# Two transformer blocks on one core: the start reordered, with the input laid out by feature and the small vectors as ready columns

## The reference

```python
def rms_norm(x, g):
    xf = x.astype(jnp.float32)
    y = xf * lax.rsqrt(jnp.mean(xf * xf, axis=-1, keepdims=True) + EPS)
    return (y * g.astype(jnp.float32)).astype(x.dtype)

hn = rms_norm(x, norm_mix_g[0])
gate, xr = jnp.split(hn @ rec_w_in, 2, axis=-1)
xpad = jnp.pad(xr, ((0, 0), (CONV_W - 1, 0), (0, 0)))
xc = conv_b + xpad[:, 0:S] * conv_w[0]
for k in range(1, CONV_W):
    xc = xc + xpad[:, k:k + S] * conv_w[k]
# then gates r, i from xc @ w_a, xc @ w_x, a scan over time, times gelu(gate), @ w_out
```

## Time and profile before

| | |
|---|---|
| median of 3 runs | 1874.32 us (1873.71 to 1875.22) |
| the profiled execution | 1874.16 us |
| its span | 1872.8 us, so 1.36 us lie around it |
| TensorE busy | 1859.4 us, 99% |
| VectorE, ScalarE, GpSimd busy | 979.5, 675.3, 377.3 us |
| DMA | 172.36 MB, mean 92 GB/s |
| granted TensorE clock | 0.999 |

### The profile page before, as it was taken

One profiled execution on the slowest core, in us unless ns is written; L12 is line 12 of the kernel. 1 busy time (PEld: TensorE's weight loads), 2 busy tenths in 40 slices (PEclk: granted clock), 3 DMA queues, 4 the chain that ended last, 5 costly groups with the idle time before them and its releaser, 6 DMA issues.

```text
span 1872.8 us, 21950 instructions
## 1 busy us (share of the span) xinstructions
PE 1859.4 (99%) x8944; PEld 1508.1 (81%) x8944; DVE 979.5 (52%) x1324; ACT 675.3 (36%) x915; POOL 377.3 (20%) x337
## 2 busy tenths in 40 slices
PE   9999999999999999999999999999999999999998
PEld 8888888888877568888888879788787888888887
DVE  7885543334458864543434356666446454443433
ACT  6753322222234772321212234555323332222213
POOL 2004210010336793210101131111001311110102
PEclk9999999999999999999999999999999999999999
DMA  4322323322333103223223232222232322233221
GB/s 160 113 90 90 113 90 101 101 90 93 104 96 96 63 1 113 91 90 112 91 90 109 80 98 84 68 68 68 85 118 80 110 93 90 90 100 103 90 96 62
DMA packets 167171, 172.36 MB, mean 92 GB/s; under 512 B 7480, under 2 KB 164288, under 8 KB 167072
## 3 DMA queue, kind: packets, MB, share of 16 engines
q1 hardware_dynamic: 164576, 163.76, 27.3%
q0 software_dynamic: 2496, 7.21, 1.2%
HBM read 168.69 MB, written 2.14 MB: 91 GB/s over the span
## 4 chain that ended last, share of the span: by engine, by line
PE 95%; ACT 2%; DVE 1%; issue 1%; DMA 0%; POOL 0%; SPq 0%; ACTq 0%
PE bank L776 30%; PE bank L778 29%; PE bank L777 29%; PE bank L801 1%; PE bank L995 1%; PE bank L1097 1%; PE bank L974 1%; PE bank L1115 1%; ACT pt L1474 0%; PE bank L923 0%; PE bank L1164 0%; PE bank L953 0%; PE bank L976 0%; DMA xtok<-in_x 0%; PE bank L1107 0%
## 5 line engine op out<-in xcount | busy, mean ns | idle before, releaser
L776 PE MATMUL bank<-Ahi,whi 128*128 128x512 f32 (+2 forms) x1416 | 552.8, 390 | 2.0 <-DVE QK L1764 1.3
L778 PE MATMUL bank<-Ahi,wlo 128*128 128x512 f32 (+2 forms) x1416 | 547.8, 387 | 0.0
L777 PE MATMUL bank<-Alo,whi 128*128 128x512 f32 (+2 forms) x1416 | 547.8, 387 | 0.0
L1752 DVE TENSOR_TENSOR wlo<-stage,whi 128x2048 fp32r<-128x2048 f32 (+2 forms) x146 | 333.1, 2281 | 379.4 <-ACT whi L1254 379.3
L1254 ACT ACTIVATE whi<-stage 128x2048 fp32r<-128x2048 f32 (+2 forms) x152 | 287.2, 1889 | 447.5 <-PE bank L778 447.5
L776 PEld LDWEIGHTS bank<-Ahi,whi 128*128 128x128 f32 (+1 forms) x1416 | 265.3, 187 | 64.6 <-issue 7.7
L778 PEld LDWEIGHTS bank<-Ahi,wlo 128*128 128x128 f32 (+1 forms) x1416 | 265.3, 187 | 55.1
L777 PEld LDWEIGHTS bank<-Alo,whi 128*128 128x128 f32 (+1 forms) x1416 | 265.4, 187 | 54.8 <-issue 1.2
L776 PE MATMUL bank<-Hhi,whi 128*128 128x512 f32 (+1 forms) x700 | 270.0, 386 | 0.0
L778 PE MATMUL bank<-Hhi,wlo 128*128 128x512 f32 (+1 forms) x700 | 269.8, 385 | 0.0
L777 PE MATMUL bank<-Hlo,whi 128*128 128x512 f32 (+1 forms) x700 | 269.8, 385 | 0.0
(11 more groups left out here) (349 smaller groups left out, 2149.1 us busy)
## 6 DMA issues: line engine op xcount, KB each, us to landing
stage<-in_mlp_w_up SPq DMA_DIRECT2D x32, 1024.0 KB, 5.3
stage<-in_mlp_w_down SPq DMA_DIRECT2D x32, 1024.0 KB, 4.9
stage<-in_w_in SPq DMA_DIRECT2D x22, 1024.0 KB, 5.1
stage<-in_w_ffn_in SPq DMA_DIRECT2D x22, 1024.0 KB, 4.9
stage<-in_w_ffn_out SPq DMA_DIRECT2D x8, 1024.0 KB, 5.1
stage<-in_rec_w_in SPq DMA_DIRECT2D x7, 1024.0 KB, 5.1
stage<-in_att_w_in SPq DMA_DIRECT2D x6, 1024.0 KB, 5.4
stage<-in_rec_w_out SPq DMA_DIRECT2D x4, 1024.0 KB, 4.8
```

The source lines that it names most:

```text
L776: e.matmul(ps, hi, rh, start=first, stop=False)
L777: e.matmul(ps, hi, rl, start=False, stop=False)
L778: return e.matmul(ps, lo, rh, start=False, stop=last)
L1752: e.tensor_tensor(lo_of(u)[:, 0:nk, 0:n], stage[s][:, 0:nk, 0:n], f32(hi_of(u)[:, 0:nk, 0:n]), ALU.subtract).then_inc(s_lo[s], 1)
```

## The change

The host hands in x transposed (`xT`, 1024 x 512) and all small vectors as one array of 128 x 153 columns (`cols`). The transposes of x, the vectors' 16 DMAs, their transposes and copies, and the ring labels of all of these go. TensorE makes 24 turns of the identity at the start instead of 13 and 10.

SP now issues, in this order: x block 0; cols; unit 0 blocks 0-1; x block 1; x 2-3; unit 0 blocks 2-3; unit 0 blocks 4-5; x 4-5; x 6-7; unit 0 blocks 6-7; unit 1 in two column halves; then units 2 onwards as before.

Unit 0 and the activations are split by feature block in 12 steps on both ACT and DVE, and `xr` 0 and 1 accumulate side by side in two banks, with 128x512 matmuls, block by block. Unit 1 is split in column halves.

The norm of layer 0 becomes like the others. POOL squares blocks 0 to 3 and sums them; ACT squares blocks 4 to 7 into `x4`, and POOL adds these. Then come `root("root_x", "rec")` on TensorE, `std_of` on ACT, and the 128x512 reciprocal on DVE.

```diff
+        load_x(0, 0, 1)
+        e.dma_start(cols[:, :], I["cols"]).then_inc(s_cols, 16)
+        load_first(0, s_load_a[0])
+        load_x(1, 1, 1)
+        load_x(2, 2, 2)
+        load_first(1, s_load_a[1])
+        load_first(2, s_load_a[2])
+        load_x(3, 4, 2)
+        load_x(4, 6, 2)
+        load_first(3, s_w[0])
+        e.dma_start(stage[1][:, :, 0:128], units[1][0][2][:, :, 0:128]).then_inc(s_load_b, 16)
+        e.dma_start(stage[1][:, :, 128:256], units[1][0][2][:, :, 128:256]).then_inc(s_w[1], 16)
+        for u in range(2, len(units)):
             load(u)
...
+        for m in range(4):
+            square("rec", m, x_there(m))
+        for m in range(4, 8):
+            e.wait_ge(s_x4, m - 3)
+            e.wait_ge(s_sq, SQ["rec"] + m)
+            e.tensor_tensor(sqa[:, :], sqa[:, :], x4[:, m - 4, :], ALU.add).then_inc(s_sq, 1)
...
+        first = [begin(("xr", m)) for m in range(2)]
+        for k in range(8):
+            if k < 6:
+                e.wait_ge(s_lo_a, k // 2 + 1)
+            else:
+                take_unit(("xr", 0))
+            e.wait_ge(s_alo, k + 1)
+            for m in range(2):
+                i = three(first[m][:, :], whi[0][:, k, m * 128:(m + 1) * 128], wlo[0][:, k, m * 128:(m + 1) * 128], Ahi[:, k, :], Alo[:, k, :], k == 0, k == 7)
+                if k == 7:
+                    i.then_inc(*ring.put(("xr", m)))
+        e.wait_ge(s_lo_b, 1)
+        product(("xr", 2), u_of["xr", 1], 0, Ahi, Alo)
+        root("root_x", "rec")
+        product(("xr", 3), take_unit(("xr", 1)), 128, Ahi, Alo)
...
+        e.wait_ge(s_cols, 16)
         first_hi(0)
+        first_weights(0, s_load_a[0], s_hi_a)
         first_hi(1)
+        first_hi(2)
+        first_weights(1, s_load_a[1], s_hi_a)
+        first_hi(3)
+        first_weights(2, s_load_a[2], s_hi_a)
+        first_hi(4)
+        first_hi(5)
+        first_hi(6)
+        first_weights(3, s_w[0], s_hi)
+        first_hi(7)
+        e.wait_ge(s_load_b, 16)
+        e.activation(whi[1][:, :, 0:128], stage[1][:, :, 0:128], ACT.Copy).then_inc(s_hi_b, 1)
+        for m in range(4, 8):
+            e.activation(x4[:, m - 4, :], X[:, m, :], ACT.Square).then_inc(s_x4, 1)
+        e.wait_ge(s_w[1], 16)
+        e.activation(whi[1][:, :, 128:256], stage[1][:, :, 128:256], ACT.Copy).then_inc(s_hi, 1)
         hi(2)
...
+        std_of("root_x", 1024)
         first_tap(0)
```

DVE's part has the same 12 steps in the same order (`first_lo(k)`: `Alo` from X and Ahi; `first_weights(i)`: `wlo` from stage and whi), then `lo` of unit 1 in halves, `lo(2)`, and:

```diff
-        e.tensor_copy(rstd[:, :], ring.bank("root_x")[:, :]).then_inc(*ring.take("root_x"))
+        root("root_x", "rec")
```

More of the change, by code:

```diff
@@ L281, in ring_mlp @@
             blocks(("dn", l, g), 8)
[L283 to L284 removed]
+    ring.add(("xr", 0), ("xr", 1), ("xr", 2), "root_x", *[("xr", m) for m in range(3, 8)])
     for m in range(4):
@@ L834, in first_root @@
-        def first_root():
-            ps = begin("root_x")
-            e.wait_ge(s_diag, 4)
-            for j in range(4):
-                t = e.matmul(ps[:, j * 128:(j + 1) * 128], ones[:, :], diag[:, j, :], start=True, stop=True)
-            t.then_inc(*ring.put("root_x"))
-        def other_columns():
-            ps = begin("v2")
-            e.wait_ge(s_v2, 16 * len(small2))
-            e.transpose(ps[:, 0:nr2], rows2[0:nr2, :], ident[0:nr2, 0:nr2]).then_inc(*ring.put("v2"))
-        def first_product(m, half):
-            cols = slice(256 * half, 256 * half + 256)
-            ps = ring.bank(("xr", m)) if half else begin(("xr", m))
-            for k in range(8):
-                if m == 0:
-                    e.wait_ge(s_alo if half else s_alo_a, k + 1)
-                i = three(ps[:, cols], whi[0][:, k, m * 128:(m + 1) * 128], wlo[0][:, k, m * 128:(m + 1) * 128], Ahi[:, k, cols], Alo[:, k, cols], k == 0, k == 7)
-            if half:
-                i.then_inc(*ring.put(("xr", m)))
@@ L1261, in std_of, with first_hi @@
             e.activation(std[:, :], ring.bank(label)[:, :], ACT.Sqrt, bias=epsc[:, 0:1], scale=1.0 / n).then_inc(*ring.take(label))
[L1263 to L1274 removed]
+        def first_hi(k):
+            e.wait_ge(*x_there(k))
+            scaled_hi(k, c0(0, k))
@@ L1769, in root @@
             e.wait_ge(s_rstd, RSTD[fill])
-        def copy_x(j):
-            label = ("x", j, 1)
-            e.wait_ge(*ring.full(label))
-            e.tensor_copy(X[:, 4:8, j * 128:(j + 1) * 128], ring.bank(label)[:, :].rearrange("p (c t) -> p c t", c=4)).then_inc(*ring.take(label))
-        def first_lo(half):
-            cols = slice(256 * half, 256 * half + 256)
-            for c in range(8):
-                e.wait_ge(s_ahi if half else s_ahi_a, c + 1)
-                e.scalar_tensor_tensor(Alo[:, c, cols], X[:, c, cols], c0(0, c), f32(Ahi[:, c, cols]), ALU.mult, ALU.subtract).then_inc(s_alo if half else s_alo_a, 1)
@@ L1792, in vector_program, with first_lo, first_weights @@
-        e.wait_ge(*ring.full("v1"))
-        e.tensor_copy(cols1[:, 0:nr1], ring.bank("v1")[:, 0:nr1]).then_inc(*ring.take("v1"))
-        copy_x(2)
-        copy_x(3)
-        first_lo(1)
-        lo(1)
+        def first_lo(k):
+            e.wait_ge(s_ahi, k + 1)
+            e.scalar_tensor_tensor(Alo[:, k, :], X[:, k, :], c0(0, k), f32(Ahi[:, k, :]), ALU.mult, ALU.subtract).then_inc(s_alo, 1)
+        def first_weights(i):
+            part = slice(2 * i, 2 * i + 2)
+            e.wait_ge(*((s_hi_a, i + 1) if i < 3 else (s_hi, 1)))
+            e.tensor_tensor(wlo[0][:, part, :], stage[0][:, part, :], f32(whi[0][:, part, :]), ALU.subtract).then_inc(s_lo_a if i < 3 else s_lo[0], 1)
@@ L1808, in vector_program @@
-        e.wait_ge(*st.now())
-        e.wait_ge(s_const, CONST["ident"])
-        for j in range(4):
-            e.tensor_scalar(diag[:, j, :], ident[:, :], ssq[:, j:j + 1], None, ALU.mult).then_inc(s_diag, 1)
-        e.wait_ge(*ring.free("v1"))
-        e.tensor_scalar(half[:, 0:16], cols1[:, r1["b_a"]:r1["b_a"] + 16], 0.5, None, ALU.mult).then_inc(s_vec, 1)
+        e.tensor_scalar(half[:, 0:16], c1("b_a", 0, 16), 0.5, None, ALU.mult).then_inc(s_vec, 1)
         lo(2)
-        e.wait_ge(*ring.full("root_x"))
```

188 lines of the change are left out of this document (54 added, 134 removed).

## The result

The changed kernel takes **1881.65 us**, the median of 5 runs (1880.26 to 1882.63), against 1874.54 for the kernel before beside it: a ratio of 1.0035 (95% interval 1.0024 to 1.0046), so 7 us slower. The forecast was 1878.6, with 1873.0 to 1881.0 as its range. The direction was right. The loss came out 3 us larger than worked out, and the time lies 0.65 us beyond the upper end of the range.

The account below looks back on a forecast made before the run. TensorE, busy 99%, was taken to bound the kernel, with DVE and ACT a rigid chain behind `rstd`. Chain +5.35 - 0.23 = +5.12, less the 0.66 margin, gave 1874.16 + 4.45 = 1878.6 us, range 1873.0 to 1881.0.

Parts of the forecast that it names:

- the turns with POOL: Start, POOL beside DVE: they alternate, 3 x 1.45 + 6 x 1.70 = 14.55 us, last-quarter `wlo` ends at 20.85, not 13.6.
- the landing of the first pieces: Start, loads: first pieces estimated in at 4.4 to 5.1 us, first collision at 6.3; landings up to 0.6 later, +0.6.
- the clock after the stall: TensorE near 47 us: a fall to its lower level would stretch `xr` 6; not in the sum, only in rival 3.
- the later need: TensorE at `ro` block 2, the product wanting `lo(11)`, 129.02 us before: forecast shift 5.12 - 0.66 = +4.45 us.
- TensorE's waits alone count, and DVE and ACT hang as one chain on `rstd`: From `shifted(0)` to `lo(11)`: a rigid chain; time is 1874.16 + chain shift - 0.66 unless TensorE comes later.
- the removed copy: One DVE copy inside the chain, 46.76 to 46.99 us, goes: -0.23 us.
- Rival 1: Start: queued DVE steps go ahead of waiting POOL, `shifted(0)` at 33.8, 1875.4 us; chance 0.17.
- Load 2 to the root: After last-quarter `wlo`: load 5.5, `hi(2)` 1.81, lambda 3.32, table load 1.28, root to first use 4.11; `shifted(0)` at 37.0.
- The two margins: TensorE's slack behind the chain's low parts: 1.6 us at `xr` 6 (`lo(3)`), 0.66 at `lo(11)`'s product.
- The stall ahead of `xr` 6: TensorE waits 4.4 us for `lo(3)`, so `xr` 6 starts at 51.15 instead of 47.42, +3.7.
- rival 3: TensorE's clock falls when fed in pairs or stalled; unit 0 and `xr` 6 stretch 2 to 4 us; 1881 to 1883; chance 0.10.
- rival 2: Start: little POOL-DVE collision, `shifted(0)` at 29.8, 1871.4 us; faster if before 32.5; chance with mixtures 0.15.

Follow-up runs that it names:

- the run without a fallen clock: Changed kernel with x blocks 0 and 1 in one load and 34 identity transposes between `xr` 5 and `xr` 6: 1878.76 us, ratio 1.0022.
- the one-load medians: Changed kernel with x blocks 0 and 1 in one 512 KB load: 1880.01 us, against 1880.74 for the changed kernel beside it.
- the run with the clock kept alone: Changed kernel with 34 transposes of the identity on TensorE between `xr` 5 and `xr` 6: 1879.82 us, ratio 1.0026.
- the kernels with their sums on TensorE: Changed kernel with squares on ACT, added by TensorE matmuls: 1873.93 us; matmuls between first products, root earlier: 1871.78; then ACT's copy before root, `lo(2)` after `shifted(0)`: 1870.08.
- the kernel with its sums late: Changed kernel with POOL's ten steps after block 0's square held until DVE's eighth low part of x: 1880.57 us, ratio 1.0032.
- the kernel without the ten steps: Changed kernel with POOL squaring only block 0 and its other ten steps left out, so another output: 1873.11 us, ratio 0.9991.

## Why the prediction was right or wrong

The mechanism that decides the sign, the turns with POOL and what is queued behind them, was right. Two terms of the sum were mis-sized: the landing of the first pieces (first collision at 6.3, measured 8.22) and the clock after the stall, which the sum put at nothing. In the profiled execution the first is most of the 1.65 us by which `shifted(0)` came after the forecast's 37.0, and the second is 2.1 us: TensorE's 8.25 at the later need, less the chain's 7.0 - 0.23 - 0.66.

- **TensorE's waits alone count, and DVE and ACT hang as one chain on `rstd`: right where the clock holds.** The table above is this claim, seven times. Where the clock fell, the chain was not rigid: DVE waited 1.3 us for `xr` 7 in the changed kernel, and `lo(11)` started 134.04 - 125.92 = 8.12 later than before, 1.35 more than `shifted(0)` and the removed copy give. TensorE itself was later still and set the time.
- **POOL and DVE exclude each other and take turns, 1.70 and 1.45 us: right.** From the first collision at 8.22 to the end of the last quarter's low part it is 14.63 us, against 14.55 worked out. In "SBUF — State Buffer", section "SBUF: two separate sides", the Trainium skill says that the holder of the shared ports keeps them for a whole instruction, and the trace agrees. Who is next, which the page leaves open, is settled for these steps: the waiting one. Rival 1, that DVE keeps its turn (1875.4), is refuted by 1.5 to 1.8 us per low part.
- **The landing of the first pieces: the step that failed first.** "An estimate from the same rate, the first pieces at 4.4 to 5.1" put the first collision at 6.3; it was at 8.22 in the profiled run, and 1.9 us late with it came everything behind. The rate of 4 MB was taken for the first pieces of 256 KB, and that was not so. In 3.75 to 5 us the DMA engines were busy half the time and moved 118 GB/s (last number of the window), in the kernel before 271; in 2.5 to 3.75 us it was 277 against 357. The range gave "landings up to 0.6 later", a third of what it needed. Why the first pieces come slowly, and not alike from run to run, stays open.

```profile
3.75:5.00 1.25, 1.25 (x7) 1.00 0.48 118
```

- **Load 2 to the root: right.** 5.2 us for the load (5.5), hi(2) 1.82 to the next start (1.81), the lambda steps 3.34 (3.32), the table load 1.28, the root to the first use 4.11 (4.11). Of the 1.4 us that a drain at the table switch would have added (the Trainium skill, "ScalarE: Activation LUTs", "What ACT_TABLE_LOAD costs") the trace shows nothing, and the measurement decides: the step before ends at 33.22, the load runs from 33.24 to 34.52, and the root starts at 34.54.
- **The two margins: right, the later one 0.1 too small.** 0.66 was taken, and 0.76 is what the run without a fallen clock shows. The stall ahead of `xr` 6 was 3.7 us against 4.4: it ended 1.5 us later than worked out (52.69 against 51.15) and began some 2.2 later (49.0 against 46.75), of which TensorE's root gives 1.2 (31.61 instead of 30.4).
- **The clock: the second step that failed, a term that the sum put at nothing.** It was named as rival 3, and given too little. It had 0.10 and "2 to 4 us" in two places. In the stretch fed in pairs the clock stayed at 1.00. At the stall it fell, in all four profiles with 3.5 us or more of waiting there. The price was 1.6 to 3.0 us of slow matmuls, of which the lead of `xr` 6 over the later need hid some 0.8. The forecast saw a stall of 4.4 us, had no row of a kernel with such a stall, and should have weighed the fall as likely. With the clock fallen its own sum would have been 1874.16 + 3.7 at `xr` 6 + 2 to 3 = 1880 to 1881. The measured 1881.65 lies in rival 3's 1881 to 1883, but not by its account alone: unit 0 kept its clock, and the late landing is part of it.
- **The miss in total.** On one chip, 1881.23 with both causes and 1878.76 without them: 2.5 us. No third loss shows, though the last 0.2 us agree partly by luck, as said above. How the 2.5 divide is settled only roughly: 0.7 by the one-load medians, within their noise, and the rest for the clock. Against the kernel before, the run with the clock kept alone stands at 1.0026, the changed kernel at 1.0034 to 1.0036, which is 1.5 to 1.9 us, with intervals that overlap.
- **The other side:** rival 2's condition, `shifted(0)` before 32.5 us, is what the kernels with their sums on TensorE meet by design.

## What to carry to other kernels

An engine with spare time is not free if its steps exclude those of the engine that feeds the critical one: ten short steps on an otherwise idle POOL cost some 8 us here (1881 against 1873), and moving them later cost as much. Eight matmuls in their place cost TensorE 1.8 us of its own, some of which lay in a stall that it had anyway. Read what waits for the *last* of the collided steps; here it was not the product but the release of a stage buffer, the next load, and ACT's queue behind it. A step that keeps TensorE ahead of a rigid chain is worth only the chain's own gain, and a stall that it opens later can take TensorE's clock down.

## What the runs showed of the hardware that I had not expected

- **The clock after a stall.** Waits of 3.5, 3.6, 3.7 and 3.8 us were each followed by a granted clock of 0.50 for 3.5 to 6 us, and one of 7.7 us (the kernel with its sums late) for some 3 us. One of 2.5 us was too, while waits of 1.3, 1.8, 2.1 and 3.2 us were not. So in this range it is not the length of the wait alone. Turns of the identity through the wait kept it at 1.00.
- **The first small loads landed late, and not always alike.** Block 1 of x, 256 KB and fourth in the queue, let POOL start at 6.6, 6.8, 7.5, 7.6, 7.9 and 8.2 us in six profiles with the same loads.
- **A mask step on POOL waits as well.** Two steps on 128x128 took 0.60 us with DVE idle for two thirds of it, and 1.63 beside DVE's last `Alo` and first half of unit 1, although they have one input. The first row is of the kernel without the ten steps, the second of the changed one:

```profile
19.18 0.60 POOL L598 TENSOR_SCALAR_AFFINE_SELECT maskf<-maskf 128x128 f32<-128x128 f32 x2
```

```profile
24.24 1.63 POOL L598 TENSOR_SCALAR_AFFINE_SELECT maskf<-maskf 128x128 f32<-128x128 f32 x2
```
